# Hyena transforms over even and odd samples, complex products on two engines, in a two-block transformer kernel

## What is computed

```python
def hyena_filter_spectra(t, z, w1, b1, w2, b2, w3, b3, sin_freq, w_out, decay):
    h = ...                                   # three sine layers of width 64
    h = (h @ w_out).reshape(L, HYENA_ORDER, 2, HYENA_WIDTH)
    h = h * exp(-t * abs(decay))
    fwd, bwd = h[:, :, 0], h[:, :, 1]
    two = concatenate([fwd, zeros, bwd[:0:-1]], axis=0)
    two = two * rsqrt(sum(two * two, axis=0))
    return rfft(two, axis=0)

def fft_long_conv(u, spec, bias):
    y = irfft(rfft(u, n=2 * L) * spec, n=2 * L)[:L]
    return y + u * bias

def hyena_mixer(u, conv_w, conv_b, spec, bias):
    u = short_conv_centred(u, conv_w, conv_b)
    parts = split(u, 3)
    z = parts[-1]
    for o in range(2):
        z = parts[o] * fft_long_conv(z, spec[:, o], bias[o])
    return z
```

## Time and profile before

| | us |
|---|---|
| median of 3 runs | 3116.73 |
| lowest to highest | 3115.55 to 3119.0 |
| the profiled execution, its own time | 3114.06 |
| its span | 3112.3 |
| mean granted clock of TensorE in it | 0.975 of full speed |
| busy: PE, DVE, ACT, POOL | 2962.5, 1201.6, 1031.6, 1162.1 |

### The profile page before, as it was taken

How to read it: one execution, slowest core, us unless ns; L and a number is a source line. 1 busy time by engine, 2 the same in 40 slices (tenths; PEclk the granted TensorE clock), 3 DMA queues, 4 the chain that set the end, 5 groups by cost and what they waited for, 6 DMA issues and landing times.

```text
span 3112.3 us, 35779 instructions
## 1 busy us (share of the span) xinstructions
PE 2962.5 (95%) x12362; PEld 2238.1 (72%) x12362; DVE 1201.6 (39%) x1941; ACT 1031.6 (33%) x1545; POOL 1162.1 (37%) x495
## 2 busy tenths in 40 slices
PE   7798899999999999899999999999999888999997
PEld 5573587888887888647536888888888544588886
DVE  4586623555535222246323222122221466432212
ACT  2226533444333322322103223233222445432222
POOL 2333462444454444303103444544445200244443
PEclk9899999999999999899999999999999888999999
DMA  5431141333332333302102333333333200132333
GB/s 133 101 95 45 57 137 55 96 94 94 101 108 88 95 100 103 131 7 83 39 0 61 95 101 94 102 102 95 101 100 103 63 21 17 38 101 95 94 102 101
DMA packets 73292, 260.33 MB, mean 84 GB/s; under 512 B 8240, under 2 KB 8752, under 8 KB 72510
## 3 DMA queue, kind: packets, MB, share of 16 engines
q1 hardware_dynamic: 66672, 242.77, 25.3%
q10 hardware_dynamic: 6542, 16.53, 2.3%
HBM read 253.24 MB, written 6.03 MB: 83 GB/s over the span
## 4 chain that ended last, share of the span: by engine, by line
PE 81%; DVE 3%; issue 3%; POOL 1%; ACT 1%; DMA 0%; DVEq 0%; POOLq 0%; ACTq 0%
PE ps L576 22%; PE ps L578 22%; PE ps L577 22%; PE ps L954 2%; PE ps L858 2%; PE ps L825 2%; PE ps L938 2%; POOL wlo L536 1%; PE ps L625 1%; PE ps L872 1%; PE ps L874 1%; DVE head_q L1797 1%; PE ps L802 1%; PE ps L811 1%; PE ps L756 0%
## 5 line engine op out<-in xcount | busy, mean ns | idle before, releaser
L536 POOL TENSOR_TENSOR wlo<-raw,whi 128x1024 fp32r<-128x1024 f32 x459 | 1123.6, 2451 | 1863.7 <-ACT whi L978 1863.4
L576 PE MATMUL ps<-lin_hi,whi 128*128 128x512 f32 x2224 | 876.3, 394 | 11.4 <-DVE lin_lo L1336 6.2
L578 PE MATMUL ps<-lin_hi,wlo 128*128 128x512 f32 x2224 | 868.4, 390 | 0.0
L577 PE MATMUL ps<-lin_lo,whi 128*128 128x512 f32 x2224 | 868.2, 390 | 0.0
L978 ACT ACTIVATE whi<-raw 128x1024 fp32r<-128x1024 f32 x459 | 481.0, 1053 | 710.2 <-PE ps L578 510.4
L576 PEld LDWEIGHTS ps<-lin_hi,whi 128*128 128x128 f32 x2224 | 419.1, 188 | 112.1 <-issue 12.4
L577 PEld LDWEIGHTS ps<-lin_lo,whi 128*128 128x128 f32 x2224 | 419.5, 189 | 88.7 <-issue 2.4
L578 PEld LDWEIGHTS ps<-lin_hi,wlo 128*128 128x128 f32 x2224 | 419.2, 188 | 88.1
L576 PE MATMUL ps<-act_hi,whi 128*128 128x512 f32 x880 | 342.6, 389 | 0.0
L578 PE MATMUL ps<-act_hi,wlo 128*128 128x512 f32 x880 | 342.4, 389 | 0.0
L577 PE MATMUL ps<-act_lo,whi 128*128 128x512 f32 x880 | 342.3, 389 | 0.0
(11 more groups left out here) (301 smaller groups left out, 2962.6 us busy)
## 6 DMA issues: line engine op xcount, KB each, us to landing
raw<-in_packs SPq DMA_DIRECT2D x459, 512.0 KB, 3.5
bias_scratch<-biasrow ACTq DMA_DIRECT2D x1, 3840.0 KB
table<-bias_scratch ACTq DMA_DIRECT2D x12, 256.0 KB, 2.7
x<-in_x_t SPq DMA_DIRECT2D x4, 512.0 KB, 8.4
out_t<-x ACTq DMA_DIRECT2D x8, 256.0 KB, 2.2
mem<-in_mem_t ACTq DMA_DIRECT2D x1, 1024.0 KB, 4.8
absdecay<-in_decay ACTq DMA_DIRECT2D x1, 1024.0 KB, 6.7
dcos<-in_dcos ACTq DMA_DIRECT2D x1, 1024.0 KB
```

The costliest lines, as they stand in the source:

```text
L536: pool.tensor_tensor(wlo[:, n % 4, :], raw[:, n % 2, :], whi[:, n % 4, :].bitcast(F32), ALU.subtract).then_inc(low_split, 1)
L576: pe.matmul(target, wh, hi[:, k, :], start=(k == 0), stop=False)
L577: pe.matmul(target, wh, lo[:, k, :], start=False, stop=False)
L578: mm = pe.matmul(target, wl, hi[:, k, :], start=False, stop=(k == total - 1))
```

## The change

Time samples are laid out with the even ones in blocks 0 and 1 and the odd ones in 2 and 3 (`every_other`). The transform of 512 samples at frequency k and at 512 - k is then the sum and the difference of an even and an odd half, so that only 256 frequencies are multiplied out: 16 matmuls per forward transform and 32 in all for the spectra. Frequency 256 is kept apart in row 0 (`middle`, eight small operations on one row, of 512 or 1024 columns, and in the products four more), and the highest one needs no column of its own in the loops. Inverse transforms likewise, by even and odd outputs; in the second order with moving operands 256 wide.

Filters: the decay row is loaded once to one partition, with `hy_wout` during ffn0's down projection, and spread by TensorE with four one-row matmuls. POOL makes `fdiff` and adds the squares over the blocks; TensorE sums them over partitions with 4 matmuls. Spectra are scaled later, by POOL, between its weight splits. In the products DVE makes the real part, POOL the imaginary one. The pool weights' matmuls come ahead of the turning, and ACT scales their results. Left out of the listing: memory offsets, names of semaphores, and waits that only follow these.

```diff
+def every_other(t):
+    at = 2 * P * (t % 2) + t // 2
+    return slice(at, at + 2 * P - 1, 2)
...
@@ def _(pool)
+        for t in range(QT):
+            pool.tensor_tensor(fdiff[:, t, :, :], both[:, :, 0, :], both[:, :, 1, :], ALU.subtract).then_inc(fdiff_ready, 1)
+            if t:
+                pool.wait_ge(filt_squared, 4 * t + 4)
+                pool.tensor_tensor(sq_sum[:, :], sq_sum[:, :], filt_sq[:, :], ALU.add).then_inc(squares_added, 1)
+        def scale_spectrum(ft, o):
+            pool.wait_ge(spec_stored, 2 * ft + o + 1)
+            order(pool.tensor_tensor(r, r, inv, ALU.mult))
+            order(pool.tensor_tensor(r, r, bias_b[:, o:o + 1, :].broadcast_to([P, 2, T]), ALU.add))
+            pool.tensor_tensor(s_, s_, inv, ALU.mult).then_inc(spec_scaled, 1)
+        for n in range(16):
+            split_low(hyena_packs + AHEAD + n, None)
+            if n % 2 and n < 8:
+                scale_spectrum(n // 4, n // 2 % 2)
+        for o in range(2):
+            for ft in range(2):
+                pool.wait_ge(even_mixed, 2 * step + 1)
+                order(pool.tensor_tensor(imag, g, spec_s[:, ft, o, :, :], ALU.mult))
+                pool.wait_ge(even_mixed, 2 * step + 2)
+                order(pool.tensor_tensor(imag_tmp[:, :, :], h, spec_r[:, ft, o, :, :], ALU.mult))
+                pool.tensor_tensor(imag_tmp[:, :, :], imag_tmp[:, :, :], imag, ALU.add).then_inc(imag_mixed, 1)
+                pool.tensor_tensor(y_all[:, ft, 2, :], imag_tmp[:, 0, :], imag_tmp[:, 1, :], ALU.add).then_inc(u_ready, 1)
...
@@ def _(pe)
+        for c in range(4):
+            pe.matmul(ps[:, 4 + c, :], ones[64:65, :], decay_row[:, c * T:(c + 1) * T], start=True, stop=True)
+        for g in range(4):
+            for part in (0, 2, 1, 3):
+                for t in (2 * odd, 2 * odd + 1):
+                    mm = pe.matmul(ps[:, 4 * (g % 2) + part, :], wave[:, t, cut], source[:, t, o, :],
+                                   start=(t % 2 == 0), stop=(t % 2 == 1))
+        pe.wait_ge(spec_stored, 3)
+        pe.wait_ge(squares_added, 3)
+        for o in range(2):
+            for side in range(2):
+                c = 2 * o + side
+                mm = pe.matmul(ps[:, 2 + o, :], ones[:, :], sq_sum[:, c * T:(c + 1) * T], start=(side == 0), stop=(side == 1))
...
+        pe.wait_ge(parts_ready, 1)
+        for g in range(4):
+            pe.matmul(ps[:, g, :], poolw[:, g, :], pooled[:, g, :], start=True, stop=True).then_inc(pool_made, 1)
-                    mm = pe.transpose(ps[:, 4 + n % 2, t * P:(t + 1) * P], src[:, c, t * P:(t + 1) * P], ident[:, :])
+                    mm = pe.transpose(ps[:, 4 + n % 4, t * P:(t + 1) * P], src[:, c, every_other(t)], ident[:, :])
+            for ft in range(2):
+                for part in (1, 0, 3, 2):
+                    for t in (2 * odd, 2 * odd + 1):
+                        mm = pe.matmul(ps[:, 4 * ((o + ft) % 2) + part, :], wave[:, t, cut], z_t[:, t, :],
+                                       start=(t % 2 == 0), stop=(t % 2 == 1))
-        project_out("pool_hyena_out", (o4_hi, o4_lo), None)
+        project_out("pool_hyena_out", (o4_hi, o4_lo), (out_ready, 8))
...
@@ def _(act)
+        def load_filter():
+            act.wait_ge(hidden_low, 2 * FC)
+            act.dma_start(hy_wout[:, :], A["fw_out"]).then_inc(wout_arrived, 16)
+            act.dma_start(decay_row, A["decay"]).then_inc(wout_arrived, 16)
+                act.activation(other[:, g % 2, k, :], ps[:, 4 * (g % 2) + part, :], ACT.Copy).then_inc(spec_copied, 1)
+                    act.activation(pooled[:, g, :], ps[:, g, :], ACT.Copy, scale=col("pool_scale", g)).then_inc(pool_scaled, 1)
+                    act.activation(odd_copy[:, ft, k, :], ps[:, 4 * ((o + ft) % 2) + part, :], ACT.Copy).then_inc(odd_copied, 1)
...
@@ def _(dve)
+                dve.tensor_tensor(spec[:, ft, o, 0, :], even, odd, ALU.add)
+                ins = dve.tensor_tensor(spec[:, ft, o, 1, :], even, odd, ALU.subtract)
+            if n in (6, 7):
+                middle(n - 6)
+                    dve.tensor_tensor(side[:, 2 * k, :], even, odd, ALU.add)
+                    dve.tensor_tensor(side[:, 2 * k + 1, :], even, odd, ALU.subtract).then_inc(even_mixed, 1)
+                order(dve.tensor_tensor(real, side[:, 0:2, :], spec_r[:, ft, o, :, :], ALU.mult))
+                order(dve.tensor_tensor(tmp[:, :, :], side[:, 2:4, :], spec_s[:, ft, o, :, :], ALU.mult))
+                order(dve.tensor_tensor(tmp[:, :, :], real, tmp[:, :, :], ALU.subtract))
+                dve.tensor_tensor(y_all[:, ft, 0, :], tmp[:, 0, :], tmp[:, 1, :], ALU.add)
+                dve.tensor_tensor(y_all[:, ft, 1, :], tmp[:, 0, :], tmp[:, 1, :], ALU.subtract).then_inc(real_ready, 1)
+                if ft == 0:
+                    order(dve.tensor_tensor(mid_x[:, :, :], side[0:1, 2:3, :].broadcast_to([1, 2, T]), mid_row[0:1, o, :, :], ALU.mult))
+                    order(dve.tensor_tensor(mid_y[:, :, :], side[0:1, 3:4, :].broadcast_to([1, 2, T]), mid_row[0:1, o, :, :], ALU.mult))
+                dve.wait_ge(imag_mixed, step + 1)
+                ins = dve.tensor_tensor(y_all[:, ft, 3, :], imag_tmp[:, 0, :], imag_tmp[:, 1, :], ALU.subtract)
...
```

More of the change, by code:

```diff
@@ L215, in build_program @@
     top8 = small[:, 56:64]
+    time_rows = small[:, 24:32]
+    neg_times = small[:, 88:92]
     put, m1 = region(big_at)
@@ L533, in _ @@
     def _(pool):
+        order = Order(pool, pool_order)
         def split_low(n, i):
@@ L557, in _ @@
+        with pool.Fori(0, (PACKS - hyena_out_packs) // 4) as i:
+            for n in range(4):
+                split_low(hyena_out_packs + AHEAD + n, i)
     @block.tensor
@@ L796, in _ @@
         pe.wait_ge(hy_act, 3)
-        def filters(t):
+        pe.wait_ge(outs_done, OUT_BASE["pool_hyena"])
+        for c in range(4):
+            pe.matmul(ps[:, 4 + c, :], ones[64:65, :], decay_row[:, c * T:(c + 1) * T], start=True, stop=True).then_inc(decay_spread, 1)
+        for t in range(QT):
             for c in range(4):
                 if t:
-                    pe.wait_ge(hy_dve, 3 + FILT_STEPS * (t - 1) + c + 1)
-                pe.matmul(ps[:, c, :], hid[:, t * P:(t + 1) * P], hy_wout[:, c * T:(c + 1) * T],
-                          start=True, stop=True).then_inc(hy_pe, 1)
@@ L805, in _ @@
-        filters(0)
-        for t in range(QT):
-            if t + 1 < QT:
-                filters(t + 1)
-            for c in range(4):
-                pe.wait_ge(hy_act, filter_squared(t, c))
-                mm = pe.matmul(ps[:, 4 + c // 2, :], ones[:, :], filt_sq[:, c * T:(c + 1) * T],
-                               start=(t == 0 and c % 2 == 0), stop=(t == QT - 1 and c % 2 == 1),
-                               skip_group_check=True)
-            mm.then_inc(hy_pe, 1)
-        pe.wait_ge(hy_arrived, 16 * HY_LOADS)
@@ L829, in _ @@
[L829 to L844 removed]
+                    pe.wait_ge(filt_made, 4 * (t - 1) + c + 1)
@@ new lines, in _ @@
+                pe.matmul(ps[:, c, :], hid[:, every_other(t)], hy_wout[:, c * T:(c + 1) * T],
+                          start=True, stop=True).then_inc(filt_summed, 1)
+        pe.wait_ge(waves_fixed, 1)
+        for g in range(4):
+            ft, o = g // 2, g % 2
+            cut = slice(ft * P, (ft + 1) * P)
+            if g >= 2:
+                pe.wait_ge(spec_stored, g - 1)
+            else:
+                pe.wait_ge(filt_made, 16) if g == 0 else pe.wait_ge(abs_ready, 4)
+            for part in (0, 2, 1, 3):
+                wave, source, odd = (cos_f, cos_f, sin_f, sin_f)[part], (fsum, fsum, fdiff, fdiff)[part], part % 2
+                pe.wait_ge(fsum_ready if part < 2 else fdiff_ready, 2 * odd + 2)
+                for t in (2 * odd, 2 * odd + 1):
+                    mm = pe.matmul(ps[:, 4 * (g % 2) + part, :], wave[:, t, cut], source[:, t, o, :],
+                                   start=(t % 2 == 0), stop=(t % 2 == 1))
+                mm.then_inc(spec_made, 1)
@@ L1679, in _ @@
-        for o in range(2):
-            dve.wait_ge(hy_pe, first + n + 1)
-            order(dve.tensor_tensor(spec_n[0:1, o, :], ps[0:1, n % 4, :], inv_norm[0:1, o, :], ALU.mult))
-            order(dve.tensor_tensor(spec_n[0:1, o, :], spec_n[0:1, o, :], bias_b[0:1, o, :], ALU.add))
-            dve.tensor_scalar(spec_n[0:1, o, :], spec_n[0:1, o, :], 1.0 / (2 * T), None, ALU.mult).then_inc(hy_dve, 1)
-            n += 1
+                    ins = dve.memset(filt[0:1, 0, cut], 0.0)
+                ins.then_inc(filt_made, 1)
```

467 lines of the change are left out of this document (282 added, 185 removed).

## The result

The changed kernel takes 3050.4 us, median of 4 runs (3049.2 to 3051.6), against 3117.0 for the kernel before (3115.6 to 3119.0) beside it: a ratio of 0.9785 with a 95% interval of 0.9774 to 0.9797. The forecast was 3058. The profiled executions have spans of 3047.3 and 3112.3 us, 65.0 apart.

The account below looks back on a forecast made before the run. TensorE, busy 95% of the span, was taken as the bound. Stages -45.3 + 29.0 - 48.8 = -65.1, less 7 us for the clock, gave -58 from 3116.7: 3058.7, rounded 3058; range 3006 to 3085, main case 3040 to 3078.

Parts of the forecast that it names:

- Stage A: Up to the first mix_w_in pack, 1301.2 to 1413.2 before; forecast to end at 1367.9, 45.3 us less.
- just hidden: POOL's differences and square sums in the filter stage: last difference at 1341.1, wanted at 1341.9.
- turn: POOL and a DVE operation with two SBUF sources exclude each other for their whole length instead of running together.
- strided accesses: Step-of-two transposing or weight-reading accesses, shown by no row: bounds 0 to 6 us, taken as 0.
- Stage B: From the first mix_w_in pack to the last conv tile: 122.3 us instead of 93.3, 29.0 more.
- a pack lands long before ACT reaches it: In mix_w_in, SP's loads come later behind POOL's splits, but weight packs still land well before ACT needs them.
- Stage C: From the last conv tile to the end of mix_w_out's first pack: 108.5 us instead of 157.3, 48.8 less.
- The clock: Slow TensorE starts after idling before the pool matmuls and in the convolutions: 1.7 to 2.2 us each, 7 in all.
- Rival 1: POOL and DVE run side by side in mix_w_in and the convolutions; 3007 us; chance 0.17.
- Rivals 2 and 3: POOL dearer by itself: 0.4 us more per instruction, 3080 (chance 0.16); added instructions at twice the price, 3125 (chance 0.05).
- Rival 4: Second order's 256-column inverse matmuls bound by weight loads: 14 us, 3068; shares the main case's chance of 0.62.

Follow-up runs that it names:

- experiment 1: Against the changed kernel, the imaginary parts of the spectrum products moved from POOL to DVE; 3033.6 us, ratio 0.9737.
- experiment 5: Against the changed kernel, POOL's three 1024-column product instructions read one tile instead of two, leaving out the multiplication by the spectrum; 3032.7 us in one run.
- experiment 2: Against the changed kernel, the twelve scalings of the spectra moved from POOL to DVE; 3048.3 us, ratio 0.9777.
- experiment 6: Against the kernel with all products on DVE, six of the middle frequency's instructions go behind the last short-convolution tile; 3029.1 us, ratio 0.9724.
- experiment 3: Against the changed kernel, imaginary products and spectrum scalings both moved to DVE, which also evicts one short-convolution tile ahead; 3030.3 us, ratio 0.9720.
- Experiment 11: Against the kernel with products and scalings on DVE, eviction ahead and middle frequency later: filter matmuls over 128 rows, zeros written behind the hidden layer; 3027.2 us.

## Why the prediction was right, and where not

**Stage A, -45.3 forecast, -46.1 measured.** Each landmark came within 1 us: filters from 1305.3 to 1332.9 (forecast 1305.6 to 1333.6), spectra to 1364.2 (1364.4), first pack at 1367.1 (1367.9). The filter matmuls stayed at 1.2 GHz, as taken from the earlier trace rows. POOL was "just hidden": its last difference ended at 1339.9 (forecast 1341.1), though at other terms: 3.3 to 3.4 us for a difference in place of 2.4. That is a turn once more, which I had not priced here: each difference was started inside DVE's sum of the same taps and ended 2.2 us after it. The last pair:

```profile
1333.66 4.03 DVE L1813 TENSOR_TENSOR fsum<-filt 128x1024 f32<-128x1024 f32 x1
1336.57 3.33 POOL L600 TENSOR_TENSOR fdiff<-filt 128x1024 f32<-128x1024 f32 x1
```

The strided accesses that no row showed cost nothing visible: 16 filter matmuls took 27.6 us where the dense price gave 28.

**Stage B, +29.0 forecast, +25.2 measured.** By its parts: DVE's pooling branch to 45.3 us after the stage's start (forecast 46), six tiles in 31.2 (33), the last six with both middles in 42.0 (42.5). (The forecast's own parts add to 121.6 and not to 122.3.) The mechanism is the one named: DVE adds of 2.78 instead of 0.72 on the chain beside scalings of 2.8. One step was wrong. I had written that "a pack lands long before ACT reaches it". ScalarE waited four times, 13.4 us, for packs to land, and one landing is on the chain (3.57 us). It cost little, since TensorE waited only 5.9 us for split weights where I had 14.6, and finished its last pack at 103.4 us (106).

**Stage C, -48.8 forecast, -46.9 measured.** 9.7 / 46.2 / 45.3 / 7.3 forecast, 10.6 / 46.8 / 44.0 / 9.0 measured. Inside the first order, the first half took 19.1 with its mixing (18.7), the second 14.2 (15.2), the last matmuls and the gate 9.6 (7.2). These last ran slow, 1.17 us each in place of 0.86. Ahead of the first half DVE had to wait for 3.9 us of forward matmuls, not 5.0.

**The clock, 7 forecast, some 7 measured.** The table of the three stretches of TensorE on the chain that began at the lower level, in the changed kernel:

```profile
1485.66:1491.20 5.54, 5.54 (x10) 2.52 (x11) 0.00 (x0) 0.00 (x0) 0.00 (x0) 0.65 0.24 92
1532.87:1538.70 5.83, 5.83 (x9) 2.53 (x10) 0.55 (x1) 0.00 (x0) 0.00 (x0) 0.62 0.00 0
1579.67:1586.00 6.33, 6.33 (x17) 5.15 (x18) 3.04 (x5) 2.19 (x4) 0.00 (x0) 0.57 0.00 0
```

The pool matmuls took 5.58 us instead of 3.5, the last matmuls of the first order 2.4 more than priced, and in the second order 16 records took 6.38 where the next 16 took 3.62. That is 2.1, 2.4 and 2.8 us, 7.3 in all. So this term was right, and the 7 us by which the spans differ from the forecast (65.0 instead of 58.1) lie elsewhere. The stages' other terms were priced too high: 0.8 us in A, 3.8 in B, and 5.4 in C, where the orders' lead and second half and the turning were shorter than forecast. Against that stand 2.8 us behind C, nearly all in the decoder's attention, where I had not looked. That the stages without the clock sum to -65.1 and the spans differ by 65.0 is luck: some 10 us of overpricing against 7 of clock and 3 of later loss. (And 3058.7 rounds to 3059, not 3058.)

**The rivals.** Rival 1 (side by side, orders of 34 us) fell by the 46.8 and 44.0 us and by experiments 1 and 5. Rivals 2 and 3 (POOL dearer by itself): POOL's products take 2.35 us when DVE is not in the way, and 3.20 beside it, which is what a turn takes, not a price of its own. Of the page that spoke against the change (the Trainium skill, GPSIMD Engine Reference, Specifications: contention for DVE instructions with two SBUF inputs, and for those in a 2-port performance mode) the runs give the size, a full turn beside a two-source instruction of POOL. I had left out the row's second condition. A DVE instruction with one SBUF source waited too (last section); it may fall under that condition, since it took 0.41 us where a two-source one of the same shape took 0.68, but no trace names the mode. Rival 4, the 256-column inverse matmuls bound by weight loads, is not seen: at full clock 16 records of them took 3.62 us, and 8 records of 512 columns, the same number of columns, 3.60.

**What I didn't see.** The prediction priced sharing the products as a gain, if a smaller one than hoped, and didn't ask what DVE would do alone. With full turns the shared form takes 2.35 and 1.24 one behind the other where DVE alone needs 1.24 and 1.24. By experiment 1 the sharing costs 11.4 us up to the decoder and 16.8 in all, more of it, by the first order, through what stands behind the products than through the products. So the 66.6 us come from the rest of the change (whose parts, the folding, the earlier loads and ScalarE's tail, no run took apart), and the sharing gave back a fifth of what there was to gain.

## What to carry to other kernels

Before work is shared between DVE and POOL, look up in the trace what a two-source DVE instruction lasts beside a two-source POOL one. Where they take turns, POOL's share must be shorter than what DVE would need for it, and for an instruction that takes DVE 1.24 us and POOL 2.35 it is not. Give POOL such work only where DVE is idle or has a source in PSUM (0.69 us beside POOL as alone). And order a pair of results so that one is finished early if TensorE can start on it: here two halves that ended together hid nothing. Count landmarks from the last point up to which two kernels are the same: without that, experiment 2's gain of 4.7 us in the mixer looks like 1.2.

## What was not expected of the hardware

- The full turn was seen only beside POOL instructions with two SBUF sources, where DVE's 1.23 us became 3.25. Beside one-source ones of as great a length DVE lost 0.7 us or nothing, and POOL's own went from 2.77 to as much as 3.7 us (experiment 5, one run).
- On DVE's side one source can be enough. A one-row multiplication by a constant (1x512, one SBUF source) took 0.41 us in experiment 6 with POOL idle, and 2.50 in experiment 3 beside a POOL split. DVE's timeline in experiment 3:

```profile
1452.05 2.50 DVE L1813 TENSOR_SCALAR spec_s<-mid_row 1x512 f32<-1x512 f32 x1
```

and in experiment 6:

```profile
1478.53 0.41 DVE L1823 TENSOR_SCALAR spec_s<-mid_row 1x512 f32<-1x512 f32 x1
```

- Sixteen matmuls of the same columns ran at a granted clock of 0.50 for 27.6 us over 64 rows, and at 0.82 and then 1.00 over 128 rows (17.6 us), with half of them zeros. Experiment 11 has the same, 17.4 us.
- A stage with the same instructions took 237.8 to 246.3 us; in the pair compared above (243.0 and 237.8) the difference was the granted clock's. Differences under 5 us between kernels of this size should be read stage by stage.
